# Reordering the end of a state-space and convolution mixer: output panels, convolution taps, expert loads and router logits

## The chip, the cores and the metric

The program runs on one core of a Trainium2 chip. A core has five engines that run side by side, each through its own list of instructions in order: PE (the matrix engine; its weight loads are shown as PEld), DVE (vector), ACT (activation functions), POOL, and SP, which here only starts transfers from device memory (DMA). They wait for each other by semaphores. The metric is the device time of one execution in microseconds (us). Before the change it is 1965.58 us, the median of three runs (1965.48 to 1965.68).

## The reference, cut to what matters

Two transformer blocks in float32 over 256 tokens of width 1024; the second block puts 16 meta tokens in front (272 rows). The change lies in the second block:

```python
proj = u @ w_in                                  # conf_a, conf_g, z, xbc, dt, gates
c = conf_a * sigmoid(conf_g)
c = depthwise_conv(c, w_conf_dw, b_conf_dw)      # 31 taps over 1024 channels
c = silu(layer_norm(c, g, b))
branch_conf = c @ w_conf_out                     # 1024 x 1024
xbc = silu(depthwise_conv(xbc, ...))             # 7 taps
y = bidir_ssd(...)                               # 4 groups of 8 heads
y = rms_norm(y * silu(z)); branch_ssm = y @ w_ssm_out     # 2048 x 1024
merged = gates[:D] * branch_conf + gates[D:] * branch_ssm
h = h + merged @ w_out
aff = softmax(rms_norm(h) @ w_router)            # 16 experts
# each expert takes its 34 tokens of highest affinity:
# gate, up (1024 x 2048 each) and down (2048 x 1024)
```

## The kernel before, in words

**Panels.** All dense products are done in panels: 128 x 2048 floats (1 MB) of weights that give 256 output channels. SP loads panel n into one of two slots as soon as panel n-2 has been used; PE does 16 products of 272 columns per panel (32 records in the trace, since each float32 product runs as two passes) into one of two PSUM pairs; ACT copies the pair out (`copy_panel`, L1257). A panel on PE waits for its slot and for the copy of panel n-2.

**The mixer of the second block.** 40 panels of `w_in_2` and `w_conf_out_2` ("mid" panels, lists `MID_OPEN`, `MID_A`, `MID_B`) are interleaved with four state-space groups. For group g PE turns x into rows (`turn_x`, L816, after DVE's `silu`, L1824), turns a small replicated tile (`turn_x0`, L822), which ACT makes in `first_rows` (L1295), forms C·B (`ssm_cb`, L829) and the outputs (`ssm_y`, L840 to L843), which need the decay masks. ACT makes these from differences and exponentials (`differences`, `cross_decays`, `own_decays`, L1303 to L1325) and DVE multiplies them (`ssm_m`, up to L1902). DVE gates y (`gated`, L1920), ACT squares and scales it (`squares`, L1335 and L1338), PE sums the squares (`ssm_sum`).

**The wide convolution.** The 31-tap convolution is 240 DVE instructions (`conf_taps`, L1810) dealt out by the table `TAPS` among the other DVE work of groups 0 to 2. When all are done (`conf_conv`), PE sums over channels (`sum_parts`, L543), DVE subtracts the mean (`centre`), ACT squares, PE sums again, ACT takes the inverse root (`norm_scale`), DVE scales (L1969), ACT applies gain and bias (L1420) and the sigmoid's logarithm, DVE and ACT finish the SiLU (L1980, `conf_ready`). Only then can the four panels of `w_conf_out_2` run; they are the last of the mid panels. Group 3 stands among these steps.

**Out of the mixer.** Eight half panels of `w_ssm_out_2` (`out_half`, L861), DVE's gating and adding of the two branches in four parts (L2000, L2002, `merged_ready`), four panels of `w_out_2`, interleaved with PE transposes of the new h (`turn_part`, L912), then the router's logits: 24 products with h as stationary operand and 16 columns moving (L922), softmax, a top-34 search on DVE, and the gather for expert 0 (L957).

**Experts.** Each of 16 experts needs 12 loads of 2 MB, dealt round a ring of 11 buffers. SP starts loads 0 to 8 among the last panels (L391), where a buffer's old content is dead, 9 and 10 after the logits, and each later one when PE has used the buffer (L418).

Of the kernel before, what the change touches and what calls it, by code (L numbers as in the profile page):

```python
# [22 lines left out]
P = 128  # L23
S = 256
META = 16
T = META + S
D = 1024
# [37 lines left out]
for _name, _count in [("w_in", 13), ("w_out", 4), ("w_up", 22), ("mid", 40), ("ssm_out", 8), ("w_out_2", 4)]:  # L65
    PANELS[_name] = _n
    _n += _count
# [3 lines left out]
def _run(kind, first, last):  # L71
# [7 lines left out]
         _run("gate", 4, 7)]  # L79
# [3 lines left out]
         _run("gate", 7, 8) + _run("out", 0, 4)]  # L83
MID = MID_OPEN + [panel for g in range(SG) for panel in MID_A[g] + MID_B[g]]
TAPS = [(0, 0, 14, 12, 14, 22), (16, 6, 16, 12, 16, 23), (16, 6, 16, 12, 16, 23)]
# [14 lines left out]
             "lgT_done": ("res_ready", 4), "lg_done": ("heads_done", 2), "lg_exp": ("raw1_ready", 1),  # L100
             "lg_shifted": ("shifted", 2), "ln_ready": ("silu_ready", 2), "m_ready": ("BT_ready", 14),
             "mean_done": ("kk_done", 2), "mean_read": ("vn1_ready", 1), "merged_ready": ("vtok_ready", 2),
             "oh_ready": ("oh_ready", 0), "oh_turned": ("kq_done", 2), "pads_ready": ("ffn_pad", 1),
             "parts_squared": ("LT_ready", 2), "pos_turned": ("o_done", 2), "rfin_ready": ("rn_ready", 1),
             "row_exp": ("ro_ln", 2), "rows_ready": ("st1_done", 1), "rst_ready": ("gsum_done", 1),
             "scattered": ("scattered", 0), "sig6": ("ro_ready", 1), "ss_ready": ("q_ready", 1),
# [8 lines left out]
def two_blocks(nc, a, out):  # L115

    with ExitStack() as ctx:
# [223 lines left out]
        def _(sp):  # L341
# [51 lines left out]
            for i in range(8):  # L393
                panel(PANELS["ssm_out"] + i)
                if i == 3:
                    sp.wait_ge(ev("ssum_done"), after["ssum_done"] + SG)
                if 3 <= i < 7:
                    expert_panel(0, i - 3)
                if i == 7:
                    expert_panel(0, 4)  # L400
                    sp.wait_ge(ev("gsig_ready"), after["gsig_ready"] + 2)
                    expert_panel(0, 5)
            for g in range(4):
                panel(PANELS["w_out_2"] + g)
                if g == 1:
                    expert_panel(0, 6)
                if g == 2:
                    sp.wait_ge(ev("merged_ready"), after["merged_ready"] + 4)
                    expert_panel(0, 7)
# [3 lines left out]
            sp.wait_ge(ev("lg_done"), after["lg_done"] + 1)  # L413
# [81 lines left out]
        def _(pe):  # L495
# [285 lines left out]
            def mid_panels(kinds):  # L781
                for kind, _ in kinds:
                    if kind == "out":
                        pe.wait_ge(ev("conf_ready"), after["conf_ready"] + 1)
                    panel(cc if kind == "out" else uT)
# [103 lines left out]
            mid_panels(MID_A[3][2:3])  # L889
            pe.wait_ge(ev("rs_ready"), 6)  # L890
            turn_x0(3)
            ssm_cb(3)
            mid_panels(MID_B[3][0:1])
            ssm_y(3)
            mid_panels(MID_B[3][1:])
            base = n[0]
            out_half(0)
            ssm_sum(3)
            for i in range(1, 8):
                out_half(i)  # L900

            pe.wait_ge(ev("merged_ready"), after["merged_ready"] + 4)
            ms_bank, lg_bank = pair[n[0] % 2][:, 0, :], pair[n[0] % 2][:, 1, :]
# [13 lines left out]
            def logits(i):  # L917

                for c in range(2 * i, 2 * i + 2):
                    for ck in (1, 2, 0):  # L920
                        t0, nt = TOK[ck]
# [1265 lines left out]
```

## Time and profile before

| | |
|---|---|
| median of three runs | 1965.58 us |
| the profiled execution | 1960.08 us |
| its span, first to last instruction | 1958.3 us |
| PE busy | 1791.8 us (91%) |
| DVE busy | 687.7 us (35%) |
| ACT busy | 594.7 us (30%) |
| read from device memory | 520.95 MB |
| granted PE clock, mean | 0.953 of full |

All stretches below are times of the profiled execution, counted from the start of its span. The second block's mid panels run from about 520 us, group 3 and the output panels from 803 to 984 us, the last four panels, router and gather to 1042 us, the experts from there to the end. "Idle" in a row is the time in which the engine did nothing before this instruction, and the name behind the arrow is what ended it. A granted clock of 1.00 is 2.4 GHz, 0.50 is 1.2 GHz.

### The profile page before, as it was taken

Reading aid. Unit: us, or ns where it says so; the run is one execution under the profiler, and the core shown is the slowest. Engines: PE = TensorE matmul, PEld = TensorE weight load, DVE = VectorE, ACT = ScalarE, POOL = GpSimd, SP = SyncE. Lnnn points to the kernel's source line nnn. Section 1 sums busy time; section 2 is a strip of 40 time slices with the busy share of each in tenths; the row PEclk is TensorE's granted clock in tenths of the full one; section 3 lists DMA queues with packets and bytes.
Section 4 is the critical chain, followed back from the end, with each engine's and each line's share of the span. In section 5 each row is a group of like instructions: output and inputs, shape, how many; then the busy total and the mean of one; then the engine's idle time right before and its main releaser. Section 6 shows DMA issues by size and latency. Waiting matters only on the chain.

```text
span 1958.3 us, 21001 instructions
## 1 busy us (share of the span) xinstructions
PE 1791.8 (91%) x8368; PEld 1049.9 (54%) x8368; DVE 687.7 (35%) x1307; ACT 594.7 (30%) x1035; POOL 19.7 (1%) x50
## 2 busy tenths in 40 slices
PE   8878789999899999689989999999988899888988
PEld 6767678888787877567773223223222232222322
DVE  0366236650358999852013211111111111111111
ACT  1142312220255735554003333222332222332222
POOL 3000000000000000000000000000000000000000
PEclk9989899999999999899999999989899999998999
DMA  4320124444244434213957999999999999999997
GB/s 168 108 86 1 38 100 155 156 155 148 107 156 153 170 112 154 87 65 108 369 214 308 428 428 427 427 428 427 428 427 428 427 427 428 427 428 428 428 427 303
DMA packets 44078, 523.29 MB, mean 267 GB/s; under 512 B 4888, under 2 KB 5080, under 8 KB 6232
## 3 DMA queue, kind: packets, MB, share of 16 engines
q1 hardware_dynamic: 42768, 511.76, 64.0%
q10 hardware_dynamic: 1224, 10.33, 1.5%
q8 instruction: 61, 1.00, 0.2%
q14 instruction: 25, 0.20, 0.0%
HBM read 520.95 MB, written 1.12 MB: 267 GB/s over the span
## 4 chain that ended last, share of the span: by engine, by line
PE 74%; DVE 13%; issue 4%; DVEq 3%; ACT 3%; DMA 3%; ACTq 0%
PE psum L1032 23%; PE psum L1004 12%; PE psum L518 11%; PE psum L776 7%; DVE arena L1810 4%; PE psum L751 4%; PE psum L1014 3%; PE psum L861 3%; DMA arena<-in_experts 2%; DVE arena L1798 2%; PE psum L733 2%; DVEq L1812 2%; PE psum L967 1%; PE psum L552 1%; PE psum L543 1%
## 5 line engine op out<-in xcount | busy, mean ns | idle before, releaser
L1032 PE MATMUL psum<-arena 128*34 128x512 f32 x2048 | 474.3, 616 | 64.5 <-issue 63.8
L776 PE MATMUL psum<-arena 128*128 128x272 f32 x1408 | 331.2, 395 | 14.7 <-DVE arena L1980 10.0
L1032 PEld LDWEIGHTS psum<-arena 128*34 128x34 f32 x2048 | 139.6, 114 | 372.6 <-issue 371.8
L776 PEld LDWEIGHTS psum<-arena 128*128 128x128 f32 x1408 | 267.9, 191 | 73.6 <-DVE arena L1980 10.4
L1509 DVE SCALAR_TENSOR_TENSOR arena<-psum,arena 34x512 f32<-34x512 f32 x64 | 44.2, 690 | 693.9 <-ACT arena L1105 693.9
L518 PE MATMUL psum<-arena 128*128 128x256 f32 x1120 | 246.5, 382 | 5.0 <-DVE arena L1525 3.9
L1004 PE MATMUL psum<-arena 128*34 128x512 f32 x1024 | 246.8, 638 | 1.2 <-ACT arena L1483 1.0
L518 PEld LDWEIGHTS psum<-arena 128*128 128x128 f32 x1120 | 213.7, 191 | 37.2 <-issue 6.6
L1004 PEld LDWEIGHTS psum<-arena 128*34 128x34 f32 x1024 | 60.8, 118 | 174.0 <-issue 171.1
L1472 ACT ACTIVATE arena<-psum 34x512 f32<-34x512 f32 x64 | 37.9, 593 | 341.1 <-PE psum L1032 341.1
L1810 DVE SCALAR_TENSOR_TENSOR arena<-arena 128x272 f32<-128x272 f32 x240 | 105.3, 499 | 4.4 <-issue 0.4
L1105 ACT ACTIVATE arena<-arena 34x512 f32<-34x512 f32 (+6 forms) x91 | 78.5, 863 | 6.9 <-issue 0.8
L751 PE MATMUL psum<-arena 128*128 128x256 f32 x352 | 76.8, 378 | 0.0
L1487 ACT ACTIVATE arena<-psum 34x512 f32<-34x512 f32 x31 | 18.3, 592 | 181.7 <-PE psum L1004 181.5
L1103 ACT ACTIVATE arena<-arena 34x512 f32<-34x512 f32 (+6 forms) x91 | 70.3, 772 | 6.2
L751 PEld LDWEIGHTS psum<-arena 128*128 128x128 f32 x352 | 66.5, 189 | 9.7
L1101 ACT ACTIVATE arena<-arena 128x512 f32<-128x512 f32 (+5 forms) x27 | 29.9, 1108 | 133.1 <-DVE arena L1744 82.9
L1111 ACT ACTIVATE arena<-arena 34x512 f32<-34x512 f32 (+2 forms) x77 | 50.2, 652 | 60.5 <-DVE arena L1509 60.5
L1798 DVE SCALAR_TENSOR_TENSOR arena<-arena 128x272 f32<-128x272 f32 x144 | 62.2, 499 | 11.6 <-ACT arena L1272 9.3
L1014 PE MATMUL psum<-arena 34*128 34x512 f32 x128 | 63.3, 635 | 0.9 <-DVE arena L2101 0.9
L861 PE MATMUL psum<-arena 128*128 128x272 f32 x256 | 59.8, 393 | 1.0 <-DMA arena<-in_panels 1.0
L2095 DVE TENSOR_TENSOR arena<-arena,psum 34x512 f32<-34x512 f32 x64 | 44.0, 687 | 44.5 <-ACT arena L1111 44.5
(383 smaller groups left out, 1449.5 us busy)
## 6 DMA issues: line engine op xcount, KB each, us to landing
arena<-in_experts SPq DMA_DIRECT2D x192, 2048.0 KB, 42.6
arena<-in_panels SPq DMA_DIRECT2D x91, 1024.0 KB, 4.9
arena<-in_down_panels SPq DMA_DIRECT2D x8, 1408.0 KB, 6.1
arena<-scr ACTq DMA_DIRECT2D x4, 2176.0 KB, 8.9
out<-arena SPq DMA_DIRECT2D x4, 256.0 KB, 2.1
arena<-in_x_cols SPq DMA_DIRECT2D x1, 544.0 KB, 4.8
arena<-in_x_cols ACTq DMA_DIRECT2D x1, 544.0 KB, 5.2
arena<-in_w_norm_final SPq DMA_DIRECT2D x1, 512.0 KB, 42.6
```

Of the source, the lines that this page charges most:

```text
L518: ins = mm(pair[k][:, b, 0:width], slot8[k][:, c, b * P:(b + 1) * P], rhs(c), start=c == 0, stop=c == DC - 1)
L751: ins = mm(G[i][:, b * S:(b + 1) * S], slot11[k][:, c, b * P:(b + 1) * P], hid[:, 11 * j + c, :], start=j == 0 and b == 0 and c == 0, stop ...
L776: ins = mm(pair[k][:, b, 0:T], slot8[k][:, c, b * P:(b + 1) * P], src[:, c, :], start=c == 0, stop=c == DC - 1)
L861: ins = mm(into[:, b, 0:T], slot8[k][:, c, b * P:(b + 1) * P], zT[:, 8 * j + c, :], start=j == 0 and c == 0, stop=j == 1 and c == DC - 1)
L1004: ins = mm(psum[64 * half:64 * half + CAP, 2, :], hx[:, f, :], r_dn[k][:, c, half * 512:(half + 1) * 512], start=f == 0, stop=f == EB - 1)
L1014: ins = mm(psum[:, 4 + 2 * tb + half, :], otT[e % 2][64:64 + CAP, tb * P:(tb + 1) * P], ysb[:, half * 512:(half + 1) * 512], start=False, ...
L1032: ins = mm(psum[lo:lo + CAP, p % 2, :], xg[:, c, :], r_up[t % RING][:, c, :], start=c == 0, stop=c == DC - 1)
L1103: A(tmp, tmp, ACT.Exp, scale=-1.0)
L1105: A(tmp, tmp, ACT.Ln, bias=ones[0:tmp.shape[0], 0:1] if one is None else one).then_inc(ev(name + "_ln"), 1)
L1111: return A(tmp if dst is None else dst, tmp, ACT.Exp)
L1798: ins = STT(gq[g % 2][:, b, :], xraw[g % 2][:, b, tap:tap + T], pcol("ssm_w", blk + 24 * tap), gq[g % 2][:, b, :], MUL, ADD)
L1810: STT(cc[:, c, :], cpad[:, c, tap:tap + T], pcol("conf_w", tap * DC + c), cc[:, c, :], MUL, ADD)
```

## The change: what it does

- The four panels of `w_conf_out_2` leave the mid panels. They now run after the eight half panels of `w_ssm_out_2`, and DVE, not ACT, takes them out of PSUM: it multiplies each by its gate and adds the state-space part.
- The 240 taps are dealt over all four groups: 62, 82, 48 and 48 in groups 0 to 3, where before groups 0 to 2 had 62, 89 and 89. The sums over channels move behind the first half panels.
- ACT's `differences(3, ..)` and `cross_decays(3)` move ahead of `squares(2)`; `first_rows(3)` stands behind both.
- ACT does both gate sigmoids and the inverse root of the state-space norm before the convolution's square; this root has its own tile and semaphore.
- The router's logits are 8 products with the router's weights as stationary operand and 272 columns moving, copied by DVE and turned by three transposes.
- SP starts expert loads 0 to 3 with half panels 4 to 7, 4 and 5 among the four conf_out panels, 6 with the second `w_out_2` panel, 7 and 8 behind the last; 9 and 10 after the new logits instead of after the old.

```diff
-         _run("gate", 4, 7)]
+         _run("gate", 4, 8)]
...
-         _run("gate", 7, 8) + _run("out", 0, 4)]
+         []]
-TAPS = [(0, 0, 14, 12, 14, 22), (16, 6, 16, 12, 16, 23), (16, 6, 16, 12, 16, 23)]
+TAPS = [(0, 0, 14, 12, 14, 22), (16, 6, 16, 12, 16, 16), (12, 4, 10, 8, 8, 6), (12, 12, 8, 16)]
...
-                if 3 <= i < 7:
-                    expert_panel(0, i - 3)
-                if i == 7:
+                if i >= 4:
+                    expert_panel(0, i - 4)
+            for g in range(4):
+                panel(PANELS["conf_out"] + g)
+                if g == 1:
                     expert_panel(0, 4)
+                if g == 2:
                     sp.wait_ge(ev("gsig_ready"), after["gsig_ready"] + 2)
                     expert_panel(0, 5)
...
             turn_x(3)
             mid_panels(MID_A[3][0:1])
+            turn_x0(3)
+            ssm_sum(2)
+            mid_panels(MID_A[3][1:2])
+            ssm_cb(3)
+            mid_panels(MID_A[3][2:])
+            ssm_y(3)
+            base = n[0]
+            out_half(0)
+            out_half(1)
+            ssm_sum(3)
             pe.wait_ge(ev("conf_conv"), after["conf_conv"] + 1)
             sum_parts(G[2], cc, DC, T).then_inc(ev("mean_done"), 1)
-            ssm_sum(2)
-            mid_panels(MID_A[3][1:2])
+            out_half(2)
             pe.wait_ge(ev("sq_ready"), SQ["conf"] + 1)
             sum_parts(G[2], conf_t, DC, T).then_inc(ev("sum_ready"), 1)
...
+            for i in range(3, 8):
                 out_half(i)
+            pe.wait_ge(ev("conf_ready"), after["conf_ready"] + 1)
+            for _ in range(4):
+                panel(cc)
...
+            def logits(first, last):
+                for c in range(first, last):
+                    ins = mm(lgT_bank[0:E, 0:T], w_r[:, c, :], hT[:, c, :], start=c == 0, stop=c == DC - 1)
...
                 copy_mid(MID_B[g][2:4])
+                if g == 2:
+                    differences(3, 0)
+                    differences(3, 1)
+                    cross_decays(3)
                 squares(g)
                 copy_mid(MID_B[g][4:])
```

Where group 3 begins, PE's list. L776 and L780 are the mid panels, L543 and L547 channel sums, L816/L818 `turn_x`, L822/L824 `turn_x0`, L829/L831 `ssm_cb`, L840/L842 the first of `ssm_y`. Before:

```order
L816 MATMUL psum<-arena 128x128 x8
L776 MATMUL psum<-arena 128x272 x16
L543 MATMUL psum<-arena 128x272 x12
L776 MATMUL psum<-arena 128x272 x16
L543 MATMUL psum<-arena 128x272 x8
L776 MATMUL psum<-arena 128x272 x16
L822 MATMUL psum<-arena 128x128 x4
L829 MATMUL psum<-arena 128x272 x3
L776 MATMUL psum<-arena 128x272 x16
L840 MATMUL psum<-arena 64x272 x2
```

The same place after:

```order
L818 MATMUL psum<-arena 128x128 x8
L780 MATMUL psum<-arena 128x272 x16
L824 MATMUL psum<-arena 128x128 x4
L547 MATMUL psum<-arena 128x272 x4
L780 MATMUL psum<-arena 128x272 x16
L831 MATMUL psum<-arena 128x272 x3
L780 MATMUL psum<-arena 128x272 x32
L842 MATMUL psum<-arena 64x272 x2
```

The sums of the convolution (8 of the first 12 in L543, and the 8 behind them) are gone from here, and `turn_x0`, with its need of ACT's tile, comes two panels sooner.

ACT's list from the last z panel's copy of group 2 on. L1257/L1260 are panel copies, L1303 to L1317 (L1306 to L1320 after) the differences and cross decays, L1335 and L1338 (L1338 and L1341) `squares`, L1295 (L1298) `first_rows`, L1411 the convolution's square. Before:

```order
L1257 ACTIVATE arena<-psum 128x544
L1335 ACTIVATE arena<-arena 128x1088
L1338 ACTIVATE arena<-arena 128x272 x4
L1295 ACTIVATE arena<-arena 128x640
L1303 ACTIVATE arena<-arena 128x128 x8
L1305 ACTIVATE arena<-arena 128x144 x8
L1257 ACTIVATE arena<-psum 128x544
L1308 ACTIVATE arena<-arena 128x128 x8
L1310 ACTIVATE arena<-arena 128x128 x8
L1411 ACTIVATE arena<-arena 128x2176
```

After:

```order
L1260 ACTIVATE arena<-psum 128x544
L1306 ACTIVATE arena<-arena 128x128 x8
L1308 ACTIVATE arena<-arena 128x144 x8
L1311 ACTIVATE arena<-arena 128x128 x8
L1313 ACTIVATE arena<-arena 128x128 x8
L1318 ACTIVATE arena<-arena 128x128 x8
L1320 ACTIVATE arena<-arena 128x144 x8
L1338 ACTIVATE arena<-arena 128x1088
L1341 ACTIVATE arena<-arena 128x272 x4
L1298 ACTIVATE arena<-arena 128x640
L1260 ACTIVATE arena<-psum 128x544
```

Six groups of eight small instructions now stand ahead of `squares(2)` and `first_rows(3)`.

PE's list from the end of the `w_out_2` panels to the logits: L912 (L916 after) is `turn_part`, L922 (L924) the logits, L934 (L935) the squares of the meta tokens, L942 (L945) the transposes of the affinities, L940 after the new transposes. Before:

```order
L912 MATMUL psum<-arena 128x128 x4
L922 MATMUL psum<-arena 128x16 x2
L922 MATMUL psum<-arena 16x16
L922 MATMUL psum<-arena 128x16 x2
L922 MATMUL psum<-arena 16x16
L912 MATMUL psum<-arena 128x128 x4
L934 MATMUL psum<-arena 16x1 x8
L922 MATMUL psum<-arena 128x16 x2
```

After:

```order
L916 MATMUL psum<-arena 128x128 x4
L924 MATMUL psum<-arena 16x272 x3
L916 MATMUL psum<-arena 128x128 x4
L935 MATMUL psum<-arena 16x1 x8
L924 MATMUL psum<-arena 16x272 x5
L940 MATMUL psum<-arena 16x16
L940 MATMUL psum<-arena 128x16 x2
L945 MATMUL psum<-arena 16x16
L945 MATMUL psum<-arena 16x128 x2
```

Behind the last row shown of before the pattern of L922 goes on to 18 products; after, five products and three transposes stand there.

## Rows read from the trace of the kernel before

**Rows 1.** The page, part 2: busy tenths of DVE in 40 slices.

```profile
DVE  0366236650358999852013211111111111111111
```

**Rows 2.** PE's waits, whole span: line, what ended it, us in total, times, longest.

```profile
PE psum L861 <- DMA arena<-in_panels: 1.0, 2, 0.8
PE psum L829 <- DVE arena L1853: 1.0, 2, 0.5
```

**Rows 3.** PE's timeline, 779 to 1001 us: start, us, line, count, [idle before <- releaser].

```profile
779.38 22.26 PE L776 MATMUL psum<-arena 128*128 128x272 f32 x96
803.35 1.09 PE L816 MATMUL psum<-arena 128*128 128x128 f32 x8 [1.70 <-DVE arena L1824]
...
825.08 8.52 PE L543 MATMUL psum<-arena 128*128 128x272 f32 x24 [13.28 <-DVEq L1812]
...
864.60 2.79 PE L840 MATMUL psum<-arena 128*64 128x272 f32 x16 [2.22 <-DVEq L1903]
...
868.61 1.57 PE L840 MATMUL psum<-arena 128*64 128x272 f32 x16
...
885.84 31.12 PE L776 MATMUL psum<-arena 128*128 128x272 f32 x128 [10.01 <-DVE arena L1980]
...
984.00 16.65 PE L776 MATMUL psum<-arena 128*128 128x272 f32 x64 [4.70 <-issue]
```

**Rows 4.** DVE's timeline: last taps, end of the convolution's SiLU, last merge.

```profile
814.60 10.40 DVE L1810 SCALAR_TENSOR_TENSOR arena<-arena 128x272 f32<-128x272 f32 x23
...
883.36 2.43 DVE L1980 TENSOR_TENSOR arena<-arena 128x2176 f32<-128x2176 f32 x1 [2.08 <-ACT arena L1287]
...
980.22 0.73 DVE L2002 TENSOR_TENSOR arena<-arena 128x544 f32<-128x544 f32 x1
```

**Rows 5.** ACT's timeline, squares(2) to the convolution's gain and bias.

```profile
814.72 1.11 ACT L1335 ACTIVATE arena<-arena 128x1088 f32<-128x1088 f32 x1 [8.57 <-DVE arena L1920]
...
818.22 2.44 ACT L1303 ACTIVATE arena<-arena 128x128 f32<-128x128 f32 x8
820.56 2.54 ACT L1305 ACTIVATE arena<-arena 128x144 f32<-128x144 f32 x8
823.00 0.61 ACT L1257 ACTIVATE arena<-psum 128x544 f32<-128x544 f32 x1
...
852.57 4.13 ACT L1420 ACTIVATE arena<-arena 128x272 f32<-128x272 f32 x8
```

**Rows 6.** Stretches: us, busy of PE, PEld, DVE, ACT, POOL, PE clock, DMA share, GB/s.

```profile
1040.00:1045.00 5.00, 3.66 (x23) 1.47 (x23) 1.97 (x6) 0.59 (x1) 0.00 (x0) 1.00 0.00 0
1200.00:1400.00 200.00, 184.11 (x816) 58.36 (x814) 34.78 (x60) 58.49 (x99) 0.00 (x0) 0.93 1.01 427
825.00:830.00 5.00, 4.92 (x11) 3.75 (x12) 2.49 (x5) 3.28 (x12) 0.00 (x0) 0.50 0.00 0
830.00:835.00 5.00, 5.00 (x21) 4.04 (x21) 3.11 (x3) 0.20 (x1) 0.00 (x0) 0.93 0.02 3
1020.00:1025.00 5.00, 5.00 (x47) 4.57 (x45) 0.31 (x2) 1.34 (x6) 0.00 (x0) 0.68 0.78 329
```

**Rows 7.** Transfers issued in 971.0 to 972.5: KB each, us from issue to landing.

```profile
arena<-in_panels SPq DMA_DIRECT2D x1, 1024.0 KB, 12.0
```

**Rows 8.** SP's first loads into freed ring buffers, and PE's last expert product.

```profile
1049.53 8.13 SPq L418 DMA_DIRECT2D arena<-in_experts  x4
...
1944.39 3.63 PE L1004 MATMUL psum<-arena 128*34 128x512 f32 x16 [0.18 <-DMA arena<-in_experts]
```

**Rows 9.** Logits to the first gather, on PE and DVE.

```profile
1020.75 6.12 PE L922 MATMUL psum<-arena 128*128 128x16 f32 x36
...
1026.92 0.26 DVE L2028 TENSOR_TENSOR arena<-psum,arena 16x16 f32<-16x16 f32 x2 [5.50 <-PE psum L922]
...
1028.85 0.71 PE L942 MATMUL psum<-arena 16*16 16x16 f32 x3 [1.97 <-DVE arena L2039]
...
1038.33 1.92 PE L957 MATMUL psum<-arena 128*34 128x512 f32 x8 [1.12 <-DVE arena L2070]
```

More of the change, by code:

```diff
@@ L64 @@
 _n = 0
-for _name, _count in [("w_in", 13), ("w_out", 4), ("w_up", 22), ("mid", 40), ("ssm_out", 8), ("w_out_2", 4)]:
+for _name, _count in [("w_in", 13), ("w_out", 4), ("w_up", 22), ("mid", 36), ("ssm_out", 8), ("conf_out", 4), ("w_out_2", 4)]:
     PANELS[_name] = _n
@@ L781, in mid_panels @@
             def mid_panels(kinds):
[L782 to L785, printed above, removed]
+                for _ in kinds:
+                    panel(uT)
             n0 = META
@@ L915, in turn_part @@
                 ins.then_inc(ev("hacc_turned"), 1)
[L917 to L921, printed above, removed]
-                        ins = mm(lg_bank[0:nt, ck * E:(ck + 1) * E], hT[:, c, t0:t0 + nt], w_r[:, c, :],
-                                 start=c == 0 and ck == 1, stop=c == DC - 1, skip_group_check=True)
+            def logits(first, last):
+                for c in range(first, last):
+                    ins = mm(lgT_bank[0:E, 0:T], w_r[:, c, :], hT[:, c, :], start=c == 0, stop=c == DC - 1)
                 return ins
@@ L929, in _ @@
                     turn_part(i - 1)
-            logits(0)
+            logits(0, 3)
             turn_part(3)
@@ L934, in _ @@
                 ins = mm(ms_bank[0:META, 0:1], sqm[:, c, :], ones[:, 0:1], start=c == 0, stop=c == DC - 1)
-            ins.then_inc(ev("lgT_done"), 1)
-            for i in range(1, 3):
-                logits(i)
-            logits(3).then_inc(ev("lg_done"), 1)
+            ins.then_inc(ev("ms_done"), 1)
+            logits(3, DC).then_inc(ev("lgT_done"), 1)
+            pe.wait_ge(ev("lgT_copied"), after["lgT_copied"] + 1)
+            for ck, (t0, nt) in enumerate(TOK):
+                ins = nc.tensor.transpose(lg_bank[0:nt, ck * E:(ck + 1) * E], left[0:E, t0:t0 + nt], ident[0:E, 0:E])
+            ins.then_inc(ev("lg_done"), 1)
             pe.wait_ge(ev("aff_ready"), after["aff_ready"] + 1)
@@ L1974, in _, with ssm_part @@
             sigmoid_arg(zt_last, zT[:, 12:16, :], "z", 4)
+            conf_taps(TAPS[3][2])
+            z_silu(3, zt_last)
+            sigmoid_arg(gate_t, gts[:, 0:DC, :], "gates", 1)
             ssm_out(3)
-            z_silu(3, zt_last)
             gated(3)
+            conf_taps(TAPS[3][3])
+            assert taps_done[0] == 240
+            dve.nop().then_inc(ev("conf_conv"), 1)
+            sigmoid_arg(gate_t, gts[:, DC:2 * DC, :], "gates", 2)
+            dve.wait_ge(ev("ssum_done"), after["ssum_done"] + SG)
+            TT(ssum, ssum, G[3][:, 0:T], ADD).then_inc(ev("ssum_ready"), 1)
+            centre()
+            base = 47 + len(MID)
+            last_of = {SSM_OUT[i][0]: base + i for i in range(8)}
+            def ssm_part(i):
+                at = last_of[i]
+                dve.wait_ge(panel_done[at % 2], at // 2 + 1)
+                part = gts[:, DC + 2 * i:DC + 2 * i + 2, :]
+                TT(part, part, pair[(base + i) % 2][:, :, 0:T], MUL).then_inc(copied[(base + i) % 2], 2)
+            dve.wait_ge(ev("gsig_ready"), after["gsig_ready"] + 2)
+            dve.wait_ge(ev("srs_ready"), after["srs_ready"] + 1)
+            TT(gts[:, DC:2 * DC, :], gts[:, DC:2 * DC, :], ssum.unsqueeze(1).to_broadcast([P, DC, T]), MUL)
+            dve.drain()
+            ssm_part(0)
+            dve.wait_ge(ev("rs_ready"), 6)
+            TT(cc, cc, rs[:, 0:T].unsqueeze(1).to_broadcast([P, DC, T]), MUL).then_inc(ev("conf_scaled"), 1)
+            ssm_part(1)
             sigmoid_arg(conf_t, cc, "conf")
```

127 lines of the change are left out of this document (49 added, 78 removed).

## The prediction

> **What bounds the kernel now.** I read the page first. DVE's slices show it full from about 600 to 820 us and nearly empty afterwards [rows 1], the end is far behind, so the question was what the rest waits for. The stretches show it: from 1050 us on the transfers run at 427 GB/s with a busy share of 1.01, while PE has idle time (184.1 busy of 200) [rows 6]. SP sends the first load into a freed ring buffer at 1049.53, and PE's last down product waits for the last load at 1944.39 [rows 8]. These are 181 loads (16 x 12 less the eleven of the first ring) of 2.097 MB; at 427 GB/s 4.91 us each, 889 us, and 1049.5 + 889 is 1938.5, the last load's landing plus some fixed latency. So the expert stage is a stream of fixed length that starts when expert 0's first products free a buffer. The stream stands still before that (0 GB/s in 1040 to 1045) [rows 6], because the ring of eleven is full. Everything that brings PE sooner to expert 0 therefore moves the whole rest by as much, as long as the ring is full by then. What counts is the time at which PE reaches expert 0, and I followed PE's timeline back from there [rows 3].
>
> Between 801.65 us (the end of 96 records from 779.38) and 984.00 PE has these gaps: 1.70 for DVE's silu(3), 13.28 for the last taps, 0.46 before a C·B product (half of the 1.0 in [rows 2]), 2.22 for the masks of group 3, 10.01 for the convolution's SiLU (`conf_ready`), 1.0 for two panel transfers [rows 2], and 4.70 before the first w_out_2 panel: 33.4 us. The last gap is merging until 980.22 + 0.73 = 980.95 [rows 4], so 1.65 after PE stopped at 979.30, and then a panel that was issued at 971.93 and took 12.0 us instead of about 5 [rows 7].
>
> **Slow starts.** After a long gap the granted clock is 0.50, the 1.2 GHz level (825 to 830), and 0.93 in the next 5 us [rows 6]. 96 records in 22.26 us [rows 3] give 0.230 us per record at the full clock. So 24 records should take 5.7 us and took 8.52 (2.8 lost), the first quarter of ssm_y lost about 1.6 (its first row is 2.79, a later one 1.57), 128 records took 31.12 instead of 29.6 (1.5), 64 took 16.65 instead of 14.9 (1.75) [rows 3]. Together 7.7 us.
>
> **The change part by part.**
>
> *Fewer taps in groups 1 and 2.* DVE does a tap in 10.40/23 = 0.452 us [rows 4]. 7 fewer in group 1 and, ahead of silu(3), 16 fewer in group 2 make silu(3) 23 x 0.452 = 10.4 us earlier; it was 1.70 late, so that gap closes, and so do the 0.50 (group 1) and 0.46 of [rows 2]. DVE then has room, and PE bounds groups 1 and 2. In group 3 DVE does 48 taps, 21.7 us; 24 of them (10.9 us) lie ahead of the masks, but 12 fall into ACT's late tile (next item) and 12 beside three panels. Hidden.
>
> *ACT's order: the new wait.* PE wants `turn_x0(3)` after turn_x(3) and one panel: 801.15 + 0.87 + 7.37 = 809.4. The tile comes from `first_rows(3)`. ACT takes the last z panel at 801.2 (0.5 until the next can start), then does six groups of eight: 2.34 us for one of 128 columns and 2.44 for one of 144, start to start [rows 5], four and two of them, 14.2 us; then squares(2) and first_rows(3), 818.22 - 814.72 = 3.5 us [rows 5]. That is 819.4, and PE waits 10.0 to 10.2 us. Behind PE's wait stand the rest of group 3 and all output panels. I take 10.2; the bounds are 7 (if ACT's small instructions ran at 0.9 of their time in the row) and 13. The start after it is slow: between 1.5 and 2.8 us by the rows above, 2.2 taken.
>
> *The convolution's sums moved.* The 13.28 goes: DVE has all taps done some 7 us before PE asks, since `gated(3)` plus 16 taps (7.2 us) end while PE runs two half panels (14.7 us). The 2.22 for the masks goes as well: from the tile on PE has 1.9 + 0.9 + 7.4 + 1.4 + 14.7 = 26 us of work before ssm_y, DVE some 22.
>
> *`conf_ready` behind eight half panels.* From the start of the mean's sum PE itself has 3.7 + 7.4 + 3.7 + 5 x 7.37 = 51.6 us before it needs `conf_ready`. The chain by rows: sum 3.7, mean and subtraction 3.0, square 2.1, wait for half panel 2 until 11.1, sum 3.7, root 1.0, scaling 2.4, gain and bias 4.1 [rows 5], logarithm 6.3, argument, exponential, product 2.4 + 2.0 + 2.4 [rows 4], and two gating steps of 0.7: about 37 us. The 10.01 goes, with 15 us to spare.
>
> *Merging and transfers.* DVE does the last gate product and addition after the last conf_out panel: 1.65 us stay, as now. Of the transfer gaps I keep 1.0: one expert load goes with each of half panels 4 to 7, where six went with half panels 3 to 7, and no panel meets two any more (the case of 12.0 us [rows 7]). Bounds 0 and 4.
>
> So gaps and slow starts of 33.4 + 5.9 become 10.2 + 2.2 + 1.7 + 1.0 = 15.1, and 0.5 came earlier: 24.7 us less until 984. With a gap of only 1.7 ahead, the w_out_2 panels keep their clock: another 1.75. Sum 26.5.
>
> *Logits.* From 1020.75 to DVE's first use at 1026.92 are 6.17 us, at a granted clock of 0.68 [rows 9, 6]. Now ten records of 272 columns, a copy of 0.43 and three transposes (0.71 for three such at the low clock [rows 9]). A record costs 0.12 by the eight of 512 columns with 34 stationary columns in 1.92 us [rows 9], scaled by columns, 0.230 by a panel, and twice that at the low clock; I take 0.18, nearer the narrow row. 1.8 + 0.2 + 0.5 + 0.7 = 3.2, a gain of 2.9, and 0.2 for the first three products: 3.1, with bounds of 0 and 4. The Trainium skill (TensorE: Matmul & The Clock Gate, Back-to-back issue gap) gives an isolated product N/2.4 + 2.5 ns at the full clock, 116 ns here; by it the ten would take 1.2 us and the gain would be 3.7. The panels' 0.230 disagrees with it, the expert rows agree.
>
> *Expert loads.* 7 goes one w_out_2 panel later, 8 stays behind the last, 9 and 10 go with the new logits. Four loads at 4.9 us are 20 us, and expert 0 frees its first buffer some 30 us after the w_out_2 panels. The stream has 9 us of stillness as cushion. Cost 0.
>
> Sum: 26.5 + 3.1 = 29.6 us. The profiled execution was 1960.1, 5.5 below the median; with its time 1930.5, and for a median 1965.6 - 29.6 = 1936.0 us.
>
> **The rivals.**
>
> *Most of the gain lost to a new wait in the convolution's chain or DVE's order.* Now the chain from the last tap (825.08) to `conf_ready` (885.79) takes 60.7 us [rows 3, 4]. If it kept that, PE would wait 60.7 - 51.6 = 9 us and start slowly (1.5): 1946.5. For it: DVE has gating steps in between that wait for PE's half panels. Against: of the 60.7 much was group 3's own work on both engines. With a second such wait at the masks, 1955.
>
> *Nothing gained:* the stream would not start sooner, since the ring is not full. Each missing load costs 4.9 us beyond the cushion of 9; it needs 8 missing loads, and only four are late at all: 1965.
>
> *Slower: the clock stays low after ACT's late tile.* The new gap of 10 us stands ahead of 16 panels without a long pause. At 0.50 eleven records took 4.92 us, 0.447 each [rows 6], 0.217 more than at the full clock, 6.9 us per panel. From 4.3 panels at the low level on the 29.6 us are gone; if all 16 ran so, the time would be 1936 + 14 x 6.9 = 2033 us. Against: after 13.28 us of idleness the clock was back within 5 to 6 us [rows 3, 6], and it returned the other three times. The Trainium skill (TensorE: Matmul & The Clock Gate, Seeing it yourself) reports a gate that was seen stuck at a low level for more than 50 us; by that rule this rival would happen, and no row here shows it.
>
> *More gained:* ACT's small instructions run faster and nothing else is late: 1930.
>
> **How the numbers follow.** Forecast 0.78 (gain 24 to 36), most of the gain lost 0.14, nothing 0.02, slower 0.05, more 0.01. What this kernel's measurement can't tell from no change is 0.2%, 4 us. Faster 0.93, same 0.02, slower 0.05. The bounds of the terms (wait 7 to 13, slow start 1.5 to 2.8, transfers 0 to 4, logits 0 to 4) give 1930 to 1945.5 if all go one way; the first rival widens it upwards, the range is 1929 to 1948.
>
> **What would show it.** Right: PE idles about 10 us before `turn_x0(3)`, released by ACT's `first_rows`; no gap over 1 us from there to the merging; a w_out_2 start at 957 to 958; SP's first ring load near 1020, and the same 909 us from there to the end. Wrong: a gap before the first conf_out panel or before the half panels 4 or 6 (DVE's gating), a granted clock of 0.5 lasting beyond 6 us, or an expert stage of another length.

## The result, and the profile after

The changed kernel takes 1930.0 us (median of four runs, 1928.9 to 1931.8), 0.9817 of the time before with a 95% interval from 0.98 to 0.9834. On another chip it took 1931.4 us (five runs) beside 1961.8 of the kernel before (nine runs): 0.9842, from 0.9829 to 0.9856. By medians that is 35.6 us on the first chip and 30.5 on the second. The changed kernel is at about the same time on both; what differs more is the kernel before, whose runs spread from 1961 to 1968 us over the chips, and on the first chip all four lay at the upper end. One run of the kernel before, beside `delay`, took 2659.9 us at a mean granted clock of 0.643 and is left out everywhere. One profiled execution against the other gives 1960.08 - 1931.83 = 28.25 us, by their spans 28.2, and as the working of the prediction was made on these, they are compared here. The forecast was 29.6 us, and a median of 1936.0 with a range from 1929 to 1948.

PE's timeline of the changed kernel from the wait for ACT's tile on (start us, us, line, count, and in brackets the idle time before and what ended it); it answers to [rows 3]:

```profile
801.38 1.03 PE L818 MATMUL psum<-arena 128*128 128x128 f32 x8
802.25 7.53 PE L780 MATMUL psum<-arena 128*128 128x272 f32 x32
819.96 2.08 PE L824 MATMUL psum<-arena 128*128 128x128 f32 x8 [10.17 <-ACT arena L1298]
821.83 3.33 PE L547 MATMUL psum<-arena 128*128 128x272 f32 x8
825.00 7.53 PE L780 MATMUL psum<-arena 128*128 128x272 f32 x32
...
872.74 5.68 PE L547 MATMUL psum<-arena 128*128 128x272 f32 x24
...
919.23 7.64 PE L863 MATMUL psum<-arena 128*128 128x272 f32 x32 [0.29 <-DMA arena<-in_panels]
926.71 29.69 PE L780 MATMUL psum<-arena 128*128 128x272 f32 x128
958.03 15.00 PE L780 MATMUL psum<-arena 128*128 128x272 f32 x64 [1.64 <-DVE arena L2015]
```

In place of the 33.4 us of gaps in [rows 3] stand three: a new one of 10.17 for ACT's `first_rows(3)` (L1298), 0.29 for a transfer, 1.64 for the merging. The first w_out_2 panel starts at 958.03, 26.0 us sooner than in [rows 3]. The 13.28 for the taps, the 2.22 for the masks and the 10.01 for `conf_ready` are gone.

ACT's queue ahead of that wait, which answers to [rows 5], and the end of the convolution's SiLU on DVE, which answers to [rows 4]:

```profile
801.58 0.63 ACT L1260 ACTIVATE arena<-psum 128x544 f32<-128x544 f32 x1 [4.76 <-PE psum L780]
802.10 2.44 ACT L1306 ACTIVATE arena<-arena 128x128 f32<-128x128 f32 x8
...
816.33 1.10 ACT L1338 ACTIVATE arena<-arena 128x1088 f32<-128x1088 f32 x1
817.51 1.76 ACT L1341 ACTIVATE arena<-arena 128x272 f32<-128x272 f32 x4
819.18 0.73 ACT L1298 ACTIVATE arena<-arena 128x640 f32<-128x640 f32 x1
```

```profile
908.04 2.43 DVE L2005 TENSOR_TENSOR arena<-arena 128x2176 f32<-128x2176 f32 x1 [2.09 <-ACT arena L1290]
911.68 0.72 DVE L1993 TENSOR_TENSOR arena<-arena,psum 128x544 f32<-128x544 f32 x1 [1.21 <-PE psum L863]
```

Six groups of small instructions, `squares(2)`, and only then the tile. `conf_ready` is done at 910.5 and PE asks for it at 926.7, with 16 us to spare.

The stretches (length, busy us of PE, PEld, DVE, ACT and POOL, then PE's granted clock, DMA share, GB/s), which answer to [rows 6]:

```profile
815.00:820.00 5.00, 0.04 (x1) 0.04 (x1) 3.12 (x8) 4.92 (x12) 0.00 (x0) 0.50 0.01 2
820.00:825.00 5.00, 5.00 (x16) 4.23 (x17) 1.29 (x2) 2.52 (x4) 0.00 (x0) 0.55 0.01 3
825.00:830.00 5.00, 5.00 (x23) 4.15 (x22) 4.65 (x11) 0.00 (x0) 0.00 (x0) 1.00 0.00 0
990.00:995.00 5.00, 5.00 (x42) 2.83 (x42) 0.63 (x3) 2.30 (x11) 0.00 (x0) 1.00 0.89 315
1010.00:1015.00 5.00, 3.66 (x18) 1.49 (x19) 1.97 (x6) 0.59 (x1) 0.00 (x0) 0.73 0.00 0
1200.00:1400.00 200.00, 180.78 (x800) 58.19 (x796) 29.50 (x56) 49.84 (x84) 0.00 (x0) 0.94 1.01 428
```

After the wait PE is at 0.50, the 1.2 GHz level, and from 825 us on at the full 2.4 GHz again. The expert stage moves 428 GB/s, where it moved 427 before. The router and expert 0, which answer to [rows 9] and [rows 8]:

```profile
993.36 2.46 PE L924 MATMUL psum<-arena 128*16 128x272 f32 x10
996.34 0.30 PE L940 MATMUL psum<-arena 16*16 16x16 f32 x3 [0.52 <-DVE arena L2039]
998.61 0.72 PE L945 MATMUL psum<-arena 16*16 16x16 f32 x3 [1.97 <-DVE arena L2054]
...
1012.18 8.77 PE L1035 MATMUL psum<-arena 128*34 128x512 f32 x32 [0.53 <-DVE arena L2090]
...
1915.88 3.63 PE L1007 MATMUL psum<-arena 128*34 128x512 f32 x16 [0.92 <-DMA arena<-in_experts]
```

```profile
1020.98 0.81 SPq L422 DMA_DIRECT2D arena<-in_experts  x2
```

The reader is to see two things. From the router's last ten records to DVE's first use of the logits pass 3.3 us (996.68 - 993.36) instead of 6.17. And SP sends the first load into a freed ring buffer at 1020.98, 28.55 us sooner than in [rows 8], although expert 0 started over 30 us sooner: its first 32 records took 8.77 us here. From 1020.98 to the end of the span are 909.1 us; before the change it was 1958.3 - 1049.5 = 908.8. This length comes back in the other profiles: it is 908.7 to 909.3 us in eleven of the fourteen, 910.1 in `delay`, and another only in `half_loads` and `hold_loads` below, which change the stream itself.

### The profile page after: what moved, and what is told of

It is laid out like the page before. It is cut to its first block, busy times and chain, and to the rows that moved or that the text cites. A ratio compares the mean times of both kernels' runs of the same rounds, so it can differ in the third digit from the quotient of the medians.

```text
span 1930.1 us, 20939 instructions
## 1 busy us (share of the span) xinstructions
PE 1781.2 (92%) x8339; PEld 1046.7 (54%) x8339; DVE 688.0 (36%) x1311; ACT 593.1 (31%) x1031; POOL 19.8 (1%) x50
## 4 chain that ended last, share of the span: by engine, by line
PE 81%; DVE 7%; issue 4%; ACT 4%; DMA 3%; DVEq 1%; ACTq 0%
PE psum L1035 23%; PE psum L1007 12%; PE psum L522 12%; PE psum L780 11%; PE psum L755 4%; PE psum L1017 3%; PE psum L863 3%; DMA arena<-in_experts 2%; PE psum L737 2%; DVE arena L1811 1%; PE psum L970 1%; PE psum L556 1%; PE psum L842 1%; PE psum L547 1%; PE psum L996 1%
## 5 line engine op out<-in xcount | busy, mean ns | idle before, releaser
L780 PE MATMUL psum<-arena 128*128 128x272 f32 x1408 | 327.9, 392 | 1.6 <-DVE arena L2015 1.6
L780 PEld LDWEIGHTS psum<-arena 128*128 128x128 f32 x1408 | 266.1, 190 | 59.0 <-DVE arena L2015 2.1
```

Source lines behind the costliest of these rows:

```text
L780: ins = mm(pair[k][:, b, 0:T], slot8[k][:, c, b * P:(b + 1) * P], src[:, c, :], start=c == 0, stop=c == DC - 1)
```

## The experiments

The theory: (1) everything that brings PE sooner to expert 0 comes out at the end one for one, since from the first freed buffer on the time is a stream of transfers of fixed length; (2) the reordering took three waits away and left one behind, which is ACT's order; (3) the taps, the logits and the expert loads bring a few microseconds each. The rivals: slack in the expert stage, most of the gain in the taps, or a convolution chain that only just fits. Differences in spans below are against the two profiles of the changed kernel, 1930.1 and 1929.4. Of medians only those go together that have about the same kernel before beside them, 1962.0 and 1961.8 for eight of the runs; beside `delay`, `half_loads`, `hold_loads` and `old_loads` it took 1964.0 (six runs).

### The changed kernel once more

No edit.

> The changed kernel once more, on the same chip as the next three. It says how far its median moves from chip to chip beside the kernel before (0.9817 of it so far), and whether expert 0's first products are at a low clock again (8.77 us in its profile, 7.08 in three of the experiments). No theory differs on it: 0.9817, 1930.

1931.4 us, 0.9842 (0.9829 to 0.9856), span 1929.4. The 0.9817 expected lies just below this interval, for the reason given above: the kernel before is faster on this chip. PE waits 10.2 us for L1298, and expert 0's first records take 8.77 us again.

### Is the new wait ACT's order?

```diff
                 arg_exp(zt, "z", g + 1, "z_exp")
+                if g == 2:
+                    first_rows(3)
                 copy_mid(MID_B[g][2:4])
...
-            first_rows(3)
             copy_mid(MID_A[3][0:1])
```

> The changed kernel with only first_rows(3) put ahead on ACT, into its idle time behind the exponential of z. My theory: PE's wait of 10.17 us before turn_x0(3) is ACT's order and goes there, but the next thing PE asks for, squares(2) for ssm_sum(2), stands in the same queue behind the same six groups of eight. It is there at 816.3 + 0.7 + 1.1 = 818.1, PE asks at 809.8 + 0.9 = 810.7: a wait of about 7.3 us before the sum, 2 to 3 us gained in all (the products of turn_x0 themselves now lie ahead of the wait), the slow start stays: 1927 against 1930. Rival (the wait is the tile's alone): all of 10.2 and the slow start, 12 us, gained: 1918.

1927.8 us, 0.9823 (0.981 to 0.9836), span 1926.3, which is 3 to 4 us less. PE's timeline:

```profile
810.03 1.05 PE L824 MATMUL psum<-arena 128*128 128x128 f32 x8
817.89 3.89 PE L547 MATMUL psum<-arena 128*128 128x272 f32 x8 [6.81 <-ACT arena L1338]
```

The tile is there in time, and PE stops one group of instructions later, for `squares(2)` from the same queue. The wait was that of ACT's queue, not the tile's alone.

```diff
                 arg_exp(zt, "z", g + 1, "z_exp")
+                if g == 2:
+                    first_rows(3)
+                    differences(3, 0)
                 copy_mid(MID_B[g][2:4])
-                if g == 2:
-                    differences(3, 0)
-                    differences(3, 1)
-                    cross_decays(3)
                 squares(g)
                 copy_mid(MID_B[g][4:])

-            first_rows(3)
+            differences(3, 1)
+            cross_decays(3)
             copy_mid(MID_A[3][0:1])
```

> The changed kernel with ACT in the order first_rows(3), differences(3, 0), copy of the z panel, squares(2), differences(3, 1), cross_decays(3). Both of PE's requests are there before it asks (squares at 804.2 by ACT's rows, PE asks at 810.6), and DVE's second half of ssm_e waits as long as now. My theory: wait 10.17 and slow start 2.3 gone, nothing else late before ssm_y, since DVE's chain to the masks has PE's 15 us of two half panels beside it, the end follows one for one: 12.5 us less, 1917.5. Rival: DVE comes late with the masks by 2 to 5 us: 1920 to 1922. Second rival: PE at full load from 780 us on gets a lower clock later and gives part of it back.

1917.6 us (1917.0 to 1919.7), 0.9773 (0.976 to 0.9786), span 1915.9. This is the fastest complete version, 13.7 us under the changed kernel by medians and 13.5 to 14.2 by spans. PE's timeline:

```profile
810.28 1.05 PE L824 MATMUL psum<-arena 128*128 128x128 f32 x8
811.17 2.00 PE L547 MATMUL psum<-arena 128*128 128x272 f32 x8
...
836.58 1.57 PE L842 MATMUL psum<-arena 128*64 128x272 f32 x16
...
914.35 20.88 PE L780 MATMUL psum<-arena 128*128 128x272 f32 x90
...
999.88 7.08 PE L1035 MATMUL psum<-arena 128*34 128x512 f32 x32 [0.53 <-DVE arena L2090]
```

ACT had stood still for 4.76 us ahead of its copy at 801.58, and the tile and `differences(3, 0)` now lie in there. Neither the masks (L842) nor the convolution (L780) comes late, both rows being without a wait (the view of the second ends within the row). More was gained than the 12.5 expected, because expert 0's first records also ran at the full clock (7.08 us). Both rivals fell: the masks aren't late, and the busier PE's mean granted clock is 0.963, beside 0.959 in the profile of the changed kernel.

### Is the slow start the clock's?

```diff
             mid_panels(MID_A[3][0:1])
+            for _ in range(11):
+                mm(G[2], ident, hTf[:, 0:512], start=True, stop=True)
             turn_x0(3)
```

> The changed kernel with eleven products of 128 x 512 without use on PE where it waits for ACT's tile: 22 records of 0.433 us, 9.5 of the 10.17 us. My theory: the 2.3 us that turn_x0(3) and ssm_sum(2) lose after the wait (2.08 + 3.33 us against 1.05 + 2.00) are the clock's, since PE stood still; with PE busy they are gone and nothing else changes: 2.3 us less. Rival (they are slow for another reason, or the products crowd out something): 0 or slower.

1928.0 us, 0.983 (0.9816 to 0.9843), span 1925.9: 3.4 to 3.5 us less than the changed kernel on the same chip, where 2.3 were expected. PE's timeline, and two stretches:

```profile
820.73 1.16 PE L824 MATMUL psum<-arena 128*128 128x128 f32 x8 [0.74 <-ACT arena L1300]
821.73 2.00 PE L547 MATMUL psum<-arena 128*128 128x272 f32 x8
...
1010.13 7.08 PE L1037 MATMUL psum<-arena 128*34 128x512 f32 x32 [0.54 <-DVE arena L2092]
```

```profile
815.00:820.00 5.00, 4.99 (x12) 1.89 (x10) 3.81 (x9) 4.92 (x14) 0.00 (x0) 1.00 0.01 2
820.00:825.00 5.00, 4.27 (x23) 3.70 (x24) 2.52 (x6) 3.29 (x6) 0.00 (x0) 1.00 0.01 3
```

The two groups behind the wait take 1.16 + 2.00 instead of 2.08 + 3.33 us, at a clock of 1.00 instead of 0.50 and 0.55. That is the slow start, shown by itself: 2.25 us. Expert 0 gave another 1.7 us, since its first records took 7.08 instead of 8.77 us. (The two make more than 3.5, because this execution came to L818 some 0.6 us later.)

### What are the taps worth?

```diff
-TAPS = [(0, 0, 14, 12, 14, 22), (16, 6, 16, 12, 16, 16), (12, 4, 10, 8, 8, 6), (12, 12, 8, 16)]
+TAPS = [(0, 0, 14, 12, 14, 22), (16, 6, 16, 12, 16, 23), (16, 6, 16, 12, 16, 23), (0, 0, 0, 0)]
```

> The changed kernel with the taps dealt as before (23 behind gated in groups 1 and 2, none in group 3). DVE comes with the argument of z at 803.2 + 1.3 instead of 795.7 as before the change, so ACT's exponential ends at 805.6 and its copy at 806.1 instead of 802.1: everything ACT does behind it, the tile for turn_x0(3) too, comes 4.1 us later. Between there and ssm_y DVE has no taps left to do and isn't late. My theory: 4 us slower than the changed kernel, 1934 (3 to 6 slower). Rival (the taps' distribution is what brings most of the gain): 13 us or more slower.

1935.5 us, 0.9865 (0.985 to 0.988), span 1933.8: 4 us slower.

```profile
805.25 1.09 PE L818 MATMUL psum<-arena 128*128 128x128 f32 x8 [1.66 <-DVE arena L1825]
...
825.83 2.08 PE L824 MATMUL psum<-arena 128*128 128x128 f32 x8 [12.11 <-ACT arena L1298]
...
1017.63 7.08 PE L1035 MATMUL psum<-arena 128*34 128x512 f32 x32 [0.54 <-DVE arena L2090]
```

The wait for silu(3) is back (1.66 us, [rows 3] had 1.70), and ACT's tile is later still. Expert 0 starts 5.45 us later, of which 1.7 come back in its first records.

### What are the logits worth?

```diff
...
-            logits(3, DC).then_inc(ev("lgT_done"), 1)
-            pe.wait_ge(ev("lgT_copied"), after["lgT_copied"] + 1)
-            for ck, (t0, nt) in enumerate(TOK):
-                ins = nc.tensor.transpose(lg_bank[0:nt, ck * E:(ck + 1) * E], left[0:E, t0:t0 + nt], ident[0:E, 0:E])
-            ins.then_inc(ev("lg_done"), 1)
+            for i in range(1, 3):
+                logits(i)
+            logits(3).then_inc(ev("lg_done"), 1)
...
```

> The changed kernel with the logits as before: 36 products of 128 x 16 behind the sum of squares instead of ten records, a copy and three transposes. My theory: the stretch from 993.36 to DVE's first use at 996.68, 3.3 us, becomes 4 to 6.2 again (6.2 with a low clock as in the profile before, less at the full one, which this stretch has now): 1 to 3 us slower, 1931 to 1933. Rival: the router has slack behind it, 0.

1933.3 us, 0.9851 (0.9836 to 0.9866), span 1931.8: 1.7 to 2.4 us slower.

```profile
992.37 5.58 PE L926 MATMUL psum<-arena 128*128 128x16 f32 x36
```

The 36 products take 5.58 us here, 6.12 in [rows 9] and 6.23 in `order_only`, the third version with the old logits. None of the three is their length at the full clock. A stretch from the midst of these products in `old_logits`, then one from the new logits in the changed kernel:

```profile
995.00:996.00 1.00, 1.00 (x7) 0.93 (x7) 0.00 (x0) 0.00 (x0) 0.00 (x0) 0.50 0.59 238
994.00:995.00 1.00, 1.00 (x6) 0.41 (x5) 0.09 (x1) 0.51 (x2) 0.00 (x0) 1.00 1.07 459
```

In all three profiles with the old logits the granted clock fell to 0.50 within 2 us of the first of the 36, although PE was busy all the time, and stayed there to the last (0.50 from 1022 to 1027 in the kernel before, from 1006 to 1011 in `order_only`); the twelve products ahead of them took 1.36 us at 1.00, so 36 would take about 4.1, an estimate. The new logits ran at 1.00 and took 2.46 us in every profile. So part of what they bring is the full clock, as far as three profiles against eleven show it; no run separates the form from the clock.

### What are the expert loads' places worth?

Here loads 0 to 3 go beside half panels 3 to 6, 4 and 5 both beside the seventh, none beside the conf_out panels, and 7 one w_out_2 panel sooner:

```diff
-                if i >= 4:
-                    expert_panel(0, i - 4)
+                if 3 <= i < 7:
+                    expert_panel(0, i - 3)
+                if i == 7:
+                    expert_panel(0, 4)
+                    sp.wait_ge(ev("gsig_ready"), after["gsig_ready"] + 2)
+                    expert_panel(0, 5)
...
```

> The changed kernel with the expert loads beside the output panels as before: loads 0 to 3 beside half panels 3 to 6, 4 and 5 both beside the seventh, 6 and 7 beside the w_out_2 panels. The first conf_out panel then queues behind three loads, as the panel issued at 971.9 did before the change (12.0 us to landing against 5). It was issued at 963.5 + 8.4 there; here PE has one panel of 7.4 us to run meanwhile, so it waits 12.0 - 7.4 = 4.6 us for it, and the clock may fall: 4 to 6 us slower, 1935. Rival: the gap is hidden, since the conf_out panels come with the convolution's 16 us of slack: 0 (this slack is DVE's, so it shouldn't help a panel).

1938.1 us, 0.9862 (0.9845 to 0.988), span 1937.8: 7.7 to 8.4 us slower by spans. PE's timeline, and the transfer times of the eight panels issued between 897 and 957 us:

```profile
931.83 32.44 PE L780 MATMUL psum<-arena 128*128 128x272 f32 x128 [4.68 <-issue]
...
1015.74 3.53 PE L960 MATMUL psum<-arena 128*34 128x512 f32 x8 [1.12 <-DVE arena L2085]
...
1021.42 7.08 PE L1035 MATMUL psum<-arena 128*34 128x512 f32 x32 [0.54 <-DVE arena L2090]
```

```profile
DMA to landing us min/median/max: 4.8/5.5/12.5
```

The gap is the 4.6 us that [rows 7] and the panel's own 7.4 gave. The cost was forecast at 4 to 6 and is larger: besides the gap 2.8 us for the four panels behind it, and, not expected, 1.6 in the gather (3.53 against 1.92 in [rows 9]). Expert 0's first records, 7.08 here against 8.77, give 1.7 of it back.

### The order alone

> The changed kernel with taps, logits and expert loads as before, so that the order of the output panels and the convolution's sums alone is new. If the parts add up, it loses what the three lost alone, by medians 5.5 + 3.3 + 8.1 = 16.9 us, by their profiles 3.7 + 1.7 + 7.7 = 13.1: 1943 to 1947, still 17 to 20 us faster than before. Rival (the order needs the others, as a wait of 13 us would be shifted and not removed): no faster than 1955.

1945.5 us (1944.3 to 1947.1), 0.9915 (0.9901 to 0.9928), span 1942.6. Its edit is the last three diffs together. By spans against 1930.1 it is 12.5 us slower than the changed kernel, where the three alone make 3.7 + 1.7 + 7.7 = 13.1; against 1929.4 it is 13.2 beside 4.4 + 2.4 + 8.4 = 15.2. Its waits in front of L824 (12.12) and L780 (4.69) are those of `old_taps` and `old_loads`. So the parts add up to within 2 us, and the order alone (PE's list with ACT's and DVE's behind it) makes 1958.3 - 1942.6 = 15.7 us. No run splits these among the three waits that it removes; that they are gone is read from the timelines.

### Is `conf_ready` 16 us early?

```diff
+            for _ in range(10):
+                A(conf_t, cc, ACT.Copy)
+                act.drain()
             sigmoid_ln(conf_t, cc, "conf")
```

> The changed kernel with ten copies without use (2.02 us each, 20.9 in a row) on ACT ahead of the convolution's SiLU. conf_ready was done at 910.5 and PE wants it at 926.7, so 16.2 us are spare. My theory: PE waits 20.9 - 16.2 = 4.7 us before the first conf_out panel and starts slowly (1.5 to 2.8 as after other gaps of 4.7): 6 to 7.5 us slower. Rival (the chain to conf_ready has little to spare, my first rival of the prediction): over 12 slower; if the spare time is larger than it looks: 0.

1941.6 us, 0.9894 (0.9879 to 0.9909), span 1937.8: 7.7 to 8.4 us slower by spans, 10.2 by medians, where 6 to 7.5 were expected. PE's timeline, then DVE's ahead of it:

```profile
930.65 32.17 PE L780 MATMUL psum<-arena 128*128 128x272 f32 x128 [5.80 <-DVE arena L1996]
...
1014.29 3.53 PE L960 MATMUL psum<-arena 128*34 128x512 f32 x8 [1.12 <-DVE arena L2088]
```

```profile
927.44 2.43 DVE L2008 TENSOR_TENSOR arena<-arena 128x2176 f32<-128x2176 f32 x1 [2.08 <-ACT arena L1290]
929.78 1.35 DVE L1996 TENSOR_TENSOR arena<-arena,psum 128x544 f32<-128x544 f32 x2
```

The copies took 20.8 us and PE waited 5.80, so 15.0 were spare and not 16.2: PE waits for the gating step that stands behind the SiLU on DVE (L1996), since it frees the PSUM pair. The panels behind the gap took 2.5 us more, as after other gaps; the 1.6 us more in the gather were not expected, as in `old_loads`. The rival (little to spare, over 12 us slower) fell.

### Is the expert stage a stream of fixed length?

```diff
             turn_gathered(0)
+            for _ in range(12):
+                mm(psum[:, 1, :], ident, ring[0][:, 0:512], start=True, stop=True)
```

> The changed kernel with 12 products of 128 x 512 without use on PE between the first gather and expert 0, 24 records of 0.433 us at the full clock (0.230 x 512/272): 10.4 us. My theory, a stream of fixed length that starts with expert 0: the end comes 10.4 us later, less up to 1.7 if expert 0's first products then run at the full clock (8.77 against 7.08 us): 8.7 to 10.4 slower. Rival (the expert stage has slack in its transfers or in PE): 0 to 5 slower.

1942.3 us (1940.1 to 1944.8), 0.989 (0.9872 to 0.9907), span 1939.2: 9.1 to 9.8 us later by spans.

```profile
1011.52 10.57 PE L989 MATMUL psum<-arena 128*128 128x512 f32 x24
1022.02 7.08 PE L1037 MATMUL psum<-arena 128*34 128x512 f32 x32
```

The first records end at 1029.03 instead of 1020.88, 8.15 us later, and the span is 9.1 longer: the whole delay arrives at the end, and a microsecond more whose cause is open. There is no slack.

```diff
-                sp.dma_start(ring[k], a["experts"][t // 12, t % 12]).then_inc(ring_loaded[k], 16)
+                if 60 <= t < 70:
+                    sp.dma_start(ring[k][:, 0:2048], a["experts"][t // 12, t % 12][:, 0:2048]).then_inc(ring_loaded[k], 16)
+                else:
+                    sp.dma_start(ring[k], a["experts"][t // 12, t % 12]).then_inc(ring_loaded[k], 16)
```

> The changed kernel with ten loads of expert 5 (the 60th to the 69th) of half the size; the other halves of these weights are those that lay in the buffers, so expert 5's result is not the reference's. My theory, transfers set the length: 10 x 4.91 / 2 = 24.5 us less, 1905.5, and PE's idle time in the stretch behind it is smaller until it has caught up. Rival (PE or its clock sets the length, since it was busy for 184 of 200 us): less than 10 gained.

This kernel leaves out half of ten loads, so expert 5 computes with other weights. 1906.4 us, 0.9704 (0.9687 to 0.9722), span 1904.8: 24.6 to 25.3 us less.

```profile
1200.00:1400.00 200.00, 193.17 (x887) 59.29 (x885) 32.71 (x57) 59.94 (x101) 0.00 (x0) 0.97 1.01 427
```

With less to wait for, PE is busy for 193 of 200 us instead of 181. The length of the stage follows its bytes: it is 885.0 us here.

```diff
-            expert_panel(0, 7)
             for last in (n[0] - 2, n[0] - 1):
                 sp.wait_ge(panel_done[last % 2], last // 2 + 1)
+            sp.wait_ge(ev("pos_turned"), after["pos_turned"] + 1)
+            expert_panel(0, 7)
             expert_panel(0, 8)
-            sp.wait_ge(ev("lgT_done"), after["lgT_done"] + 1)
```

> The changed kernel with loads 7 to 10 of expert 0 held back until the positions are turned (about 1007 us). The stream then runs from 1007 without a standstill: 185 loads of 4.91 us from 1007.0 instead of 181 from 1020.9, so the end is 1007.0 + 908.4 against 1020.9 + 888.7, 5.8 us later: 1936. Rival (four loads fit in PE's slack): 0. It sizes the cushion of 13 us: three loads would have been free.

1937.4 us, 0.9862 (0.9844 to 0.9879), span 1934.9: 4.8 to 5.5 us slower, where 5.8 were expected. The loads go out at 1006.52 and the queue never stands still:

```profile
1006.52 0.80 SPq L392 DMA_DIRECT2D arena<-in_experts  x2
1007.37 37.58 SPq L422 DMA_DIRECT2D arena<-in_experts  x10
```

From there 185 loads of 4.91 us against 181 from 1020.98 is 5.2 us by the measured times. The cushion is as large as it looked, and a late load costs only what goes beyond it.

## Why the prediction was right

*The number (within the range, by 1 us).* On the profiled executions 29.6 us were forecast and 28.2 came. The median of 1930.0 lies 6.0 below the forecast, next to the lower bound of 1929, and on the 1930 of the last rival; but that rival's cause did not come, as ACT's groups took 2.44 us, the same as in [rows 5]. The forecast took 29.6 from the 1965.6 of the first chip, while its working was made on an execution of 1960.1. From the 1961.8 of the other chip the same working gives 1932.2, and 1931.4 was measured. That the first chip's median stayed in the range was partly luck.

*The bound (right).* The expert stage is 909 us from the first freed buffer, before and after and in nine other profiles, and it follows its start (`delay`) and its bytes (`half_loads`). This also closes the rival in which the stream would not start sooner.

*The new wait (right).* 10.0 to 10.2 us were forecast and 10.17 came; `rows_only` and `rows_first` show that it is ACT's order. The working missed that the same rows showed how to be rid of it.

*The slow start behind it (right).* 2.2 forecast, 2.25 by `warm`. The rival of a clock that stays low did not come: the stretch 825 to 830 is at 1.00. The gate stuck low for over 50 us that the Trainium skill reports (TensorE: Matmul & The Clock Gate, Seeing it yourself) did not appear: the slow time ended about 5 us after PE's first product at 819.96.

*The convolution (right).* The sums and `conf_ready` cost no wait. The chain took 36 us where 37 were forecast. The 15 us to spare are 15.0 by `conf_late`; the gating step behind the SiLU, which the working had in its 37 us, is the true end of the chain.

*Transfers (term mis-sized).* 1.0 was kept and 0.29 came. The bound of 4 and the slow start behind it, put down to [rows 7], is where the edit of the loads earns its part: `old_loads` shows a gap of 4.68 and 7.7 us in all.

*Taps (right in sum).* The gaps of 1.70, 0.50 and 0.46 closed. Undoing the edit costs about 4 us and not 2.7, since DVE's taps also held back the exponential that ACT's queue starts with; that was already in the 10.2 us, where ACT was taken to start at 801.2.

*Logits (term mis-sized).* 6.17 became 3.3 us as forecast, but only 1.7 to 2.4 us are the edit's. The low clock of [rows 6] was there in all three profiles with the old logits and in none with the new; where it sets in differs (6.12, 5.58 and 6.23 us for the same 36 products), and with it what the edit is worth. A record of 272 columns with 16 stationary columns took 2.46/10 = 0.246 us and not the 0.18 used; the copy and the transposes took less than was set aside for them, as they ran at the full clock. The records with 16 stationary columns cost about what a panel's cost, so the 116 ns worked out from the Trainium skill (TensorE: Matmul & The Clock Gate, Back-to-back issue gap) aren't a record's. The Trainium skill (FP8 and Floating Point Precision, TensorE Precision Notes) says that a true float32 product makes four passes through the array; as an estimate, four times 116 ns are 0.46 us, which is the two records of 0.230 that a product has here. The description of the kernel before calls the two records two passes; the traces show only that each product has two records. The 0.12 came from rows of another kind: expert 0's records of 512 columns take 7.08/32 = 0.221 us, while those of 512 columns with 128 stationary columns take 9.61/22 = 0.437 in `warm`. The gather's and the experts' products write to two separate groups of PSUM rows, from 0 and from 64, and the logits' don't; that this halves their time isn't tested.

*Not foreseen: 1.7 us given back at expert 0.* PE reached expert 0 30.25 us sooner (1042.43 to 1012.18), a little more than the sum. Its first 32 records then took 8.77 us, at a granted clock of 0.73 in 1010 to 1015, where the kernel before took 7.08 at 1.00 in [rows 6]. So 28.55 us remain at the first freed buffer and 28.2 at the end. The forecast of 29.6 had no term for it; that it came so close to 28.2 is in part because PE reached expert 0 0.65 us sooner than forecast.

The parts as the experiments give them, by spans against 1930.1: order 15.7, loads 7.7, taps 3.7, logits 1.7, together 28.8 against 28.2 measured. Expert 0's first records gave 1.7 us back in `old_taps`, `old_loads` and `order_only` and not in `old_logits`, so each part is known to a microsecond or two.

## What to carry to other kernels

When a reordering takes PE's waits away, list what PE asks for next from each engine's queue, in order, and look for idle time of that engine ahead of the request: here ACT stood still for 4.76 us and then made masks nobody needed yet, and moving its blocks gave another 14 us, half of what the whole change did. Where the rest of a program is a stream that starts with one event, cost every edit by the time of that event alone, and check that transfers are ahead of it. Price a wait of PE at its length plus the slow products behind it: of 4.7 us `old_loads` made 7.7, and of 10.2 `rows_first` got back 14, of which 1.7 came from expert 0's first records.

## What was not expected of the hardware

In the three profiles with the old logits the granted clock falls to 0.50 in the midst of them, while PE is busy all the time; in the kernel before its last wait longer than half a microsecond had ended 38 us earlier, at 984.00. What brings it down there stays open.

Expert 0's first 32 records took either 8.77 or 7.08 us, always the same two values. They took 8.77 in both profiles of the changed kernel and in `rows_only`, `old_logits`, `hold_loads`, `half_loads` and `conf_late`, and 7.08 in `rows_first`, `warm`, `old_taps`, `old_loads`, `order_only` and `delay`. In `old_loads` and `conf_late` the gather ahead of them took 3.53 us instead of 1.92. In these two the 14 records of filler products in front of the gather (L949) took 6.17 us, in all others 7.3 to 8.2. There DVE's search for the positions runs beside them, so most of a slow stretch costs nothing, while in the gather and at expert 0 all of it is paid. Somewhere between the logits and expert 0 the clock falls for some microseconds, and an event 190 us earlier moves the place: `warm` changes nothing between the wait at 810 and the gather but the 2.25 us and the busy PE. It isn't simply the absence of an earlier wait, since `old_taps` and `order_only` have the longest (12.11 and 12.12) and the fast value. (In `delay` the fast value isn't comparable, as products without use stand right ahead.) What sets the place stays open; it makes a difference of 1.7 us between versions, about as much as the new logits bring.
